# First attention of a two-block network: the softmax-share transpositions move to the head of each step, and one copy moves ahead of a weight split

## The reference

```
def softmax_attend(q, k, v, scale):                       # 8 "mla" heads
    s = einsum('bqhd,bkhd->bhqk', q, k) * scale
    return einsum('bhqk,bkhd->bqhd', softmax(s), v)
# 8 "swa" heads: keys are context + a band of the image tokens (masked), and a sink
p = softmax(concatenate([s_ctx, s_band, sink_col], -1))
o = einsum(p_ctx, v_ctx) + einsum(p_band, v_band)
out = concatenate([o_mla, o_swa], -1) @ w_out
gates = split(silu(cond) @ w_mod + b_mod, 6)              # modulation, six vectors
```

## Time and profile before

| what | value |
|---|---|
| median of three runs | 1531.13 us (1530.96 to 1533.8) |
| the profiled execution's own time | 1531.83 us |
| its span in the trace | 1530.0 us |
| PE busy | 1490.3 us, 97% of the span |
| DVE, ACT busy | 851.4 us, 742.2 us |
| first attention | from about 96 us to 218 us of the span |

### The profile page before, as it was taken

How to read it: one execution, slowest core, us unless ns; L and a number is a source line. 1 busy time by engine, 2 the same in 40 slices (tenths; PEclk the granted TensorE clock), 3 DMA queues, 4 the chain that set the end, 5 groups by cost and what they waited for, 6 DMA issues and landing times.

```text
span 1530.0 us, 25220 instructions
## 1 busy us (share of the span) xinstructions
PE 1490.3 (97%) x10318; PEld 1157.5 (76%) x10318; DVE 851.4 (56%) x1519; ACT 742.2 (49%) x1184; POOL 1.4 (0%) x6
## 2 busy tenths in 40 slices
PE   7999999999999999999999999999999999999986
PEld 5655567777887888789968899998998899534442
DVE  2457767744334444673597765768588875222213
ACT  3545663644223332362464764545655644555444
POOL 0000000000000000000000000000000000000000
PEclk9999999999999999999999999998999999999999
DMA  9412543243233332543226346534453357999995
GB/s 389 186 52 102 202 150 126 110 165 128 88 130 115 133 112 76 184 151 110 99 85 251 133 159 220 179 133 146 168 175 135 123 185 277 423 427 426 427 428 229
DMA packets 36374, 288.24 MB, mean 188 GB/s; under 512 B 4112, under 2 KB 4240, under 8 KB 11552
## 3 DMA queue, kind: packets, MB, share of 16 engines
q1 hardware_dynamic: 35936, 285.93, 49.6%
q0 software_dynamic: 176, 0.59, 0.1%
q10 hardware_dynamic: 144, 0.06, 0.0%
HBM read 285.51 MB, written 1.05 MB: 187 GB/s over the span
## 4 chain that ended last, share of the span: by engine, by line
PE 85%; DMA 6%; DVE 5%; ACT 2%; issue 1%; DVEq 0%; SPq 0%; ACTq 0%
PE ps L582 19%; PE ps L583 18%; PE ps L584 18%; PE ps L3239 7%; DMA deep<-wts 5%; PE ps L634 2%; PE ps L1758 1%; PE ps L1656 1%; PE ps L1729 1%; PE ps L3115 1%; PE ps L1828 1%; PE ps L1827 1%; PE ps L1826 1%; DVE WL L567 1%; PE ps L2099 1%
## 5 line engine op out<-in xcount | busy, mean ns | idle before, releaser
L582 PE MATMUL ps<-HH,WH 128*128 128x512 f32 (+2 forms) x944 | 324.8, 344 | 1.3 <-DVE WL L567 1.2
L567 DVE TENSOR_TENSOR WL<-ring,WH 128x2048 fp32r<-128x2048 f32 (+2 forms) x134 | 281.1, 2102 | 71.7 <-ACT WH L557 71.7
L583 PE MATMUL ps<-HL,WH 128*128 128x512 f32 (+2 forms) x944 | 320.4, 339 | 0.0
L584 PE MATMUL ps<-HH,WL 128*128 128x512 f32 (+2 forms) x944 | 320.1, 339 | 0.0
L557 ACT ACTIVATE WH<-ring 128x2048 fp32r<-128x2048 f32 (+2 forms) x134 | 236.1, 1764 | 123.5 <-PE ps L584 108.9
L582 PEld LDWEIGHTS ps<-HH,WH 128*128 128x128 f32 (+1 forms) x944 | 179.2, 190 | 35.1 <-issue 12.9
L584 PEld LDWEIGHTS ps<-HH,WL 128*128 128x128 f32 (+1 forms) x944 | 179.1, 190 | 20.1
L583 PEld LDWEIGHTS ps<-HL,WH 128*128 128x128 f32 (+1 forms) x944 | 179.3, 190 | 18.8 <-issue 0.2
L3239 PE MATMUL ps<-deep,arena 128*32 128x512 f32 (+1 forms) x808 | 114.9, 593 | 9.0 <-ACT other_b L3225 5.2
L582 PE MATMUL ps<-UHL,WH 128*128 128x256 f32 (+3 forms) x416 | 120.4, 289 | 0.0
L582 PE MATMUL ps<-parts,WH 128*128 128x512 f32 (+1 forms) x352 | 119.2, 339 | 0.6 <-DVE WL L567 0.6
(11 more groups left out here) (468 smaller groups left out, 2474.0 us busy)
## 6 DMA issues: line engine op xcount, KB each, us to landing
ring<-wts SPq DMA_DIRECT2D x128, 1024.0 KB, 4.9
deep<-wts SPq DMA_DIRECT2D x39, 2048.0 KB, 18.5
ring<-wts SPq DMA_DIRECT2D x32, 704.0 KB, 4.0
arena<-wts SPq DMA_DIRECT2D x13, 1024.0 KB, 12.6
under_x<-wts SPq DMA_DIRECT2D x6, 2048.0 KB, 21.6
deep<-wts SPq DMA_DIRECT2D x9, 1024.0 KB, 9.1
ring<-wts SPq DMA_DIRECT2D x4, 672.0 KB, 13.5
X<-xin SPq DMA_DIRECT2D x4, 512.0 KB, 16.3
```

The source lines that it names most:

```text
L567: e.tensor_tensor(lo, raw(i), hi.bitcast(F32), ALU.subtract).then_inc(*up("low", i))
L582: e.matmul(o, w[0][:, cols], x[0], start=k == 0, stop=False)
L583: e.matmul(o, w[0][:, cols], x[1], start=False, stop=False)
L584: return e.matmul(o, w[1][:, cols], x[0], start=False, stop=k == nk - 1)
```

## The change

Two edits. In `pe_heads` the share transposition gets a function of its own, `pe_share`, which PE calls as the first thing of step i for unit i-3; before, it came after that unit's value products. `pe_share` now takes the output bank of the unit, and the signal `values` is raised by the last value product. In `dve_heads`, for the modulation steps after step 20, `dve_turn` stands ahead of `dve_mod`.

```diff
             for i in range(len(UNITS) + 3):
+                if 0 <= i - 3:
+                    pe_share(e, i - 3)
                 if i < len(UNITS):
                     pe_scores(e, i)
...
-                if i in MODS_AT:
+                if i in MODS_AT and i <= 20:
                     dve_mod(e, 0, MODS_AT[i])
                 for j in turned_at(i):
                     dve_turn(e, j)
+                if i in MODS_AT and i > 20:
+                    dve_mod(e, 0, MODS_AT[i])
...
         def pe_values(e, j):
-            b = banks.of["o", ot, lat] if lat and qt else bank(e, "o", ot, lat)
+            b = banks.of["o", ot, lat]
...
+            t.then_inc(*up("values", j))
+            if not lat or qt:
+                banks.give(b, "o_unit", ot, lat)
+
+        def pe_share(e, j):
+            kind, p, lat, qt = UNITS[j]
+            ot = out_tile(UNITS[j])
+            b = banks.of["o", ot, lat] if lat and qt else bank(e, "o", ot, lat)
             e.wait_ge(*at("exp.share", j))
             for q in range(query_tiles(j)):
                 c = 256 + 128 * (qt + q)
-                t = e.transpose(ps[:, b, c:c + 128], WIDE[j % 2][q], ident)
-            t.then_inc(*up("values", j))
-            if not lat or qt:
-                banks.give(b, "o_unit", ot, lat)
+                e.transpose(ps[:, b, c:c + 128], WIDE[j % 2][q], ident)
```

More of the change, by code:

```diff
@@ L1757, in pe_values @@
                     v = VM[:, vt, 64 * h:64 * h + 64] if kind == "mla" else VS[:, vt, 64 * s:64 * s + 64]
-                    e.matmul(ps[64 * s:64 * s + 64, b, 128 * qt:128 * qt + nq], v, PTA[:, j % 2, s, nq * kt:nq * kt + nq],
-                             start=kt == 0, stop=kt == nk - 1)
+                    t = e.matmul(ps[64 * s:64 * s + 64, b, 128 * qt:128 * qt + nq], v,
+                                 PTA[:, j % 2, s, nq * kt:nq * kt + nq], start=kt == 0, stop=kt == nk - 1)
+            t.then_inc(*up("values", j))
[5 more added lines that the diff above has]
+            b = banks.of["o", ot, lat] if lat and qt else bank(e, "o", ot, lat)
             e.wait_ge(*at("exp.share", j))
```

## The result

| what | before | after |
|---|---|---|
| median, 20 runs each | 1531.9 us (1529.71 to 1534.18) | 1534.72 us (1532.03 to 1537.69) |
| ratio after to before, 95% interval | | 1.0018 [1.0012, 1.0024] |
| the profiled execution's own time | 1531.83 us | 1535.26 us |
| its span | 1530.0 us | 1533.5 us |
| PE busy | 1490.3 us | 1490.9 us |

The changed kernel is 0.18% slower, 1.8 to 3.7 us: the direction and the range of the prediction, and 2 us above its single value, 0.8 of which is the median of before, 1531.9 here against the 1531.13 that the prediction started from. It is also above what the forecast by itself allowed (1532.0 to 1533.9) and where its rival "slower" put the time (1534.4 to 1535): the range holds it because the range took that rival in. In the changed kernel ACT's share L1718 is L1722 and its copy L1743 is L1747.

What follows compares the result with a forecast made beforehand. PE's throughput was taken to bound most of the stage, a DVE-ACT chain its last third. ACT 0.7 us later put PE's restart 1.6 us later: 1531.83 + 1.6 = 1533.4, as a median 1532.7 us; range 1530.2 to 1535.2.

Steps and rivals of the forecast that it cites:

- the forecast by itself: The main case without rivals: 1.6 us lost at the last step, time 1532.0 to 1533.9 us, chance 0.54.
- rival "slower": Longer gap ahead of the restart keeps PE's clock low twice as long, another 1.7 us lost: 1534.4 to 1535; chance 0.20.
- sign of being right: L1762 behind L1775, longest wait for ACT's L1718, L1741 before L567, step 20 scores wait for L1695, L648 1 to 3 us later.
- The chain up to unit 23: Unit 23's exponentials come 0.2 - 0.5 + 0.5 + 0.5 = 0.7 us later, and what ACT does behind them.
- Scores of step 9: Early steps: 0.16 won in step 3's wait, 0.4 lost to L1488's bank; 0.2 us lost taken, 0.2 won to 0.4 lost.
- Steps 9 to 16: Eight PE-bound steps where share transpositions cost less in their new place: 0.5 us won, from 0 to 1.2.
- The unknown of the prediction: Whether value products directly followed by modulation products pay the shape change that stood behind the share; if so, nothing is saved.
- Banks: Step 20's scores wait for the bank released by unit 19's first head's exponentials: 0.5 us late, between 0 and 0.8.
- The restart: Last step: PE waits for ACT's L1718 of unit 23 and restarts at 217.8 instead of 216.24, 1.6 us lost.
- From the restart on, PE has the same products ahead of it: Step from restart to L648: same products, only shares before values, so the restart's 1.6 us delay is the loss.
- rival "faster": Unit 23's shares ready at about 214.3, so the 1.9 us wait and 1.7 us low-clock loss go: 1527.0; chance 0.06.
- low clock at another place: Sign of being wrong: PE's granted clock falls somewhere other than behind the last wait of the stage; no size given.

Runs made afterwards that it cites:

- e3: Changed kernel, but in the last step unit 23's value products stand ahead of its shares; ratio to before 0.9993 [0.9985, 1.0002].
- e4: Changed kernel, but the shares stand behind the scores and ahead of the values, banks handed out as before; ratio to before 1.0007 [0.9998, 1.0016].
- e5: Changed kernel, with unit 23's share ahead of the weight splits of step 24 on DVE and ACT; ratio to before 0.9994 [0.9984, 1.0004].
- e6: Changed kernel, but shares behind the modulation products, ahead of the turns; unit 23's share and L660 moved ahead of splits; 1527.62 us, ratio to before 0.9973.
- e7: Changed kernel, but shares in the place of before; unit 23's share ahead of the splits, L660 ahead of the second; 1527.76 us, ratio to before 0.9972.
- e2: Kernel before with only DVE's new order (copy ahead of the weight split), shares where they were; ratio to before 0.9987 [0.9978, 0.9995].
- e1: Changed kernel with DVE's order as before, so only the shares moved; ratio to before 1.0020 [1.0011, 1.0029].

## Why the prediction was right, and what was mis-sized

All places are relative to the first L1525, so that the 0.51 us by which after's stage begins later is taken out.

**The mechanism holds.** L1762 of unit 23 starts behind L1775, the longest wait of PE is for ACT's share, L1741 runs ahead of L567, the scores of step 20 wait, and L648 comes 1.84 us later: each sign of being right that the prediction named. e3 shows that the order of values and share in the last step is the main cause: with that order alone undone the loss is gone. The size of 1.6 us was too small, and the steps below say where.

**The chain up to unit 23.** Its exponentials start at 115.68 instead of 115.01: 0.67 later, 0.7 predicted. The sum is right by two errors that cancel. Scores of step 9: predicted 0.2 late, measured 48.77 against 47.79, 0.98 late. Of this, 0.11 is one more share that now stands ahead of them. In step 3 the predicted bank wait of L1488 is there (0.29 of idle time, and the product starts 0.46 later). The share that fills PE's wait there wins 0.17 behind the values, and the share of unit 1 ahead of the next scores takes it back, so that these are 0.50 late. The rest comes a tenth a step (step 4 to step 5: 5.71 us, 5.59 before). Steps 9 to 16 then gain 38.88 - 37.89 = 1.0, where I took 0.5 from between 0 and 1.2. At the scores of step 17 the two kernels are level (86.66 against 86.67), as they were in the prediction's sum: 0.2 lost, 0.5 won, about 0.3 lost to the shares ahead of the scores. What these steps look like now, PE in order of time, and then the value products of step 12 before, against the earlier trace rows:

```profile
158.01 1.09 PE L1762 MATMUL ps<-arena 128*64 128x128 f32 x16
159.04 1.07 PE L634 MATMUL ps<-ring,scond 128*32 128x512 f32 x8
160.03 1.09 PE L1733 MATMUL ps<-cst,arena 128*128 128x128 f32 x8
160.96 0.27 PE L1775 MATMUL ps<-cst,arena 128*128 128x128 f32 x1
161.07 0.38 PE L1654 MATMUL ps<-cst 128*128 128x128 f32 x2
```

```profile
157.13 1.09 PE L1758 MATMUL ps<-arena 128*64 128x128 f32 x16
```

The share takes 0.11 (160.96 to 161.07), and value products directly followed by modulation products take 1.03 (158.01 to 159.04), as ahead of a share before (157.13 to 158.15, 1.02). The unknown of the prediction, whether the change of shape would cost there what it cost behind the share, is answered: on average 0.12 of the 0.15 us is saved in each of these steps. The Trainium skill, TensorEngine Tiling (Array Packing), Key Properties, says that a change of the tiling mode drains the engine; the rows agree in kind, since the share costs 0.26 between two other shapes and 0.11 among its own.

**Banks.** PE, step 20, and ACT's last row for unit 19's first head, against the earlier trace rows:

```profile
191.86 0.38 PE L1775 MATMUL ps<-cst 128*128 128x128 f32 x2
192.56 1.13 PE L1662 MATMUL ps<-arena 64*128 64x256 f32 x8 [0.32 <-issue]
...
192.27 0.19 ACT L1699 ACTIVATION_READ_ACCUMULATOR arena<-ps,small 128x1 f32 x1
```

The scores are 0.49 later than before (99.48 against 98.99), where 0.5 was taken from 0 to 0.8; 0.32 of it is idle time. The row names no releaser, but ACT's row ends at 192.46, a tenth before the scores start. In e4, which gives the scores their old bank, they start at 192.26 while the same row of ACT there ends at 192.77: it is the bank. What is left of the 0.67, some 0.2, arises in steps 21 to 23, where about 0.3 was worked out.

**The restart.** Predicted 1.6 us later, measured 124.99 against 123.67, 1.32 later. ACT's share started 0.10 later (124.32 against 124.22) where 0.4 was worked out: it no longer waits for DVE, as said, but L660 ended 0.54 later and not 0.7 (124.45 against 123.91), and the share begins before L660's recorded end, at 217.40 against 217.53, where I had let it start at that end.

**The step that was mis-sized** is "From the restart on, PE has the same products ahead of it". The products are the same, their clock is not. The stretches in which PE restarted, before (at 216.24) and after (at 218.07):

```profile
216.00:217.00 1.00, 0.76 (x6) 0.68 (x8) 0.72 (x4) 0.70 (x2) 0.00 (x0) 0.85 0.76 123
```

```profile
218.00:219.00 1.00, 0.93 (x4) 0.59 (x6) 0.42 (x1) 0.51 (x2) 0.00 (x0) 0.50 0.58 213
```

Before, PE's clock was still at 0.85 on average in that microsecond; after, it stood at 0.50 already. From the restart to L648 that makes 2.50 us instead of 1.98, so L648 is 1.84 late and not 1.32. (In e4, with after's order in this step and a clock of 0.71 in the microsecond of its restart, it is 2.22.) And in two of three executions the low clock then lasted twice as long: 3.4 us are lacking instead of 1.7, and the stage is 1.4 and 1.3 us longer than in the first. That is about the 1.7 us of the rival "slower"; its condition, low for more than 6 us behind the restart, is met in the second execution (6.2) and just missed in the third (5.8), where the clock fell 1.0 us ahead of the restart. In the mean of the three executions the stage is 2.2 us longer: 1.8 up to L648 and 0.3 behind it, where the mean of after (12.67) is little above that of before (12.36).

**Where the time could have gone instead.** The rival "faster" said that the time falls if unit 23's share is ready before about 215. e5 moves it ahead of the splits and gains, but less than the 4 us named there: its median is 1531.0, with an interval of its ratio that takes in 1. The stage is 1.5 us shorter than before; the next late copy, L660, and the early steps keep the rest. With L660 moved too, and the shares not at the step's head, 4.5 us appear (e6, e7); no run tells these two steps apart.

**What stays open**: why the low stretch lasts once or twice as long behind the same wait. And whether the change has a part in the 0.8 us behind the stage. The prediction called low clock at another place a sign of being wrong, and from 1514 to 1520 us the clock is 0.86, 1.00 and 0.74 in after's three executions and 1.00 in all of before. But e2 and e4 have such a fall there too, and e1, which has the shares at the step's head as after does, has none.

## What to carry to other kernels

When a wait is to be removed, look for the second latest thing behind the same stop: here the copy from DVE was 1.9 us late and the share from ACT later still, and the values that had covered the share were put behind it. On an engine that works in order, what is moved to the head of a step must be ready first, and it also takes its bank first; the work whose operands are ready earliest belongs ahead. The lasting gain (0.27%) came from the engines that were late: short copies that PE waits for go ahead of the weight splits of 1.9 us on ACT and 2.3 us on DVE, one after another until the stop at the end of the stage is gone.

## What was not expected of the hardware

Waits of PE of 0.83, 1.25 and 1.50 us at this place (e5, e3, e2) were followed by no fall of its granted clock, waits of 1.92, 2.21 and 2.63 us (before, after and e4, e1) went with a fall to 0.50, up to 1.2 us ahead of the restart or up to 0.7 us behind it. The rest of the 13 traces says nearly the same: from 30 us on none of the 23 waits of PE of 1.4 to 1.85 us had a fall beside it, and 13 of the 15 waits of 1.92 us or more had one; 2.14 us in before (at 1426 us) and 2.68 us in e1 (at 1490 us) had none. A long wait is not the only occasion either: near 1050 us the clock fell in 9 of the 13 executions, where PE's waits were all under 0.5 us.

What the fall at the end of the stage cost was 1.7 us in before, after and e4, and 3.4 us in e1 and in two of the three executions of after, so one execution doesn't tell what such a wait costs: in the same kernel the clock lacked 1.7 us more or less with L648 at the same place within 0.01 us.
